# A chain of seven transformer blocks: the end of each block cut by token halves, and the next block begun on the first half

## What is computed

```
x = layer_norm(ALPHA * x + 0.5 * swiglu(x, gate, up, down))    # "ffn1"
mix = rwkv7_mix(x @ w_in)  or  stick_breaking_mix(x @ w_in), with memory_attention
x = layer_norm(ALPHA * x + heads @ w_out)                      # output stage
x = layer_norm(ALPHA * x + 0.5 * swiglu(x, gate, up, down))    # "ffn2"

def layer_norm(x, g, b):
    mu, var = mean(x), mean((x - mu)**2)
    return (x - mu) * rsqrt(var + 1e-5) * g + b                # over the 1024 channels
```

## Time and profile before

| | us |
|---|---|
| median of 3 runs | 1715.24 (1713.86 to 1715.44) |
| the profiled execution | 1710.65 |
| its span, first to last instruction | 1709.0 |
| PE busy in the span | 1482.6 (87%) |
| DVE, ACT, POOL busy | 1030.7, 677.7, 221.7 |
| mean granted TensorE clock | 0.924 |

### The profile page before, as it was taken

One profiled execution on the slowest core, in us unless ns is written; L12 is line 12 of the kernel. 1 busy time (PEld: TensorE's weight loads), 2 busy tenths in 40 slices (PEclk: granted clock), 3 DMA queues, 4 the chain that ended last, 5 costly groups with the idle time before them and its releaser, 6 DMA issues. The chain is left out here.

```text
span 1709.0 us, 29899 instructions
## 1 busy us (share of the span) xinstructions
PE 1482.6 (87%) x11905; PEld 1351.6 (79%) x11905; DVE 1030.7 (60%) x1264; ACT 677.7 (40%) x826; POOL 221.7 (13%) x213
## 2 busy tenths in 40 slices
PE   6768698999899997883886899979999796789996
PEld 5564577999799996883885799979999795589996
DVE  5499956666655556567554655565555646465555
ACT  3355155444443333553232333334333345233332
POOL 0067202222110002101221100001000002110000
PEclk9889788999999998996998899989999898789998
DMA  9655444666476663420003566637666341366661
GB/s 300 195 170 185 142 136 136 185 184 184 123 215 185 186 187 104 149 99 1 4 3 123 173 184 184 185 110 225 186 186 189 99 148 50 123 181 187 185 186 47
DMA packets 318908, 257.42 MB, mean 151 GB/s; under 512 B 7089, under 2 KB 298487, under 8 KB 318839
## 3 DMA queue, kind: packets, MB, share of 16 engines
q1 hardware_dynamic: 318839, 256.44, 49.9%
HBM read 255.36 MB, written 1.05 MB: 150 GB/s over the span
## 5 line engine op out<-in xcount | busy, mean ns | idle before, releaser
L133 PE MATMUL ps<-actT,a_parts 128*128 128x256 f32 x2192 | 634.2, 289 | 51.0 <-DVE a_parts L118 30.1
L134 PE MATMUL ps<-actT,a_parts 128*128 128x256 f32 x2192 | 631.1, 288 | 0.0
L135 PE MATMUL ps<-actT,a_parts 128*128 128x256 f32 x2192 | 630.4, 288 | 0.0
L133 PEld LDWEIGHTS ps<-actT,a_parts 128*128 128x128 f32 x2192 | 432.0, 197 | 62.4 <-issue 33.0
L134 PEld LDWEIGHTS ps<-actT,a_parts 128*128 128x128 f32 x2192 | 432.1, 197 | 3.9
L135 PEld LDWEIGHTS ps<-actT,a_parts 128*128 128x128 f32 x2192 | 431.6, 197 | 0.0
L969 DVE TENSOR_TENSOR a_parts<-a_raw,a_parts 128x2048 fp32r<-128x2048 f32 x100 | 240.4, 2404 | 76.7 <-ACT a_parts L966 76.7
L980 DVE TENSOR_TENSOR b_parts<-b_raw,b_parts 128x1024 fp32r<-128x1024 f32 x80 | 98.1, 1226 | 173.9 <-ACT b_parts L977 173.9
L118 DVE TENSOR_TENSOR a_parts<-a_raw,a_parts 128x2048 fp32r<-128x2048 f32 x54 | 127.3, 2361 | 106.0 <-ACT a_parts L114 105.9
L966 ACT ACTIVATE a_parts<-a_raw 128x2048 fp32r<-128x2048 f32 x100 | 190.0, 1900 | 0.5 <-DMA a_raw<-in_ffn_w_up 0.5
L977 ACT ACTIVATE b_parts<-b_raw 128x1024 fp32r<-128x1024 f32 x100 | 105.7, 1057 | 185.8 <-PE ps L135 185.8
(11 more groups left out here) (305 smaller groups left out, 1634.8 us busy)
## 6 DMA issues: line engine op xcount, KB each, us to landing
a_raw<-in_ffn_w_gate SPq DMA_DIRECT2D x88, 512.0 KB, 3.9
a_raw<-in_ffn_w_up SPq DMA_DIRECT2D x88, 512.0 KB, 5.1
b_raw<-in_ffn_w_down SPq DMA_DIRECT2D x88, 512.0 KB, 3.5
arena<-in_mod_w SPq DMA_DIRECT2D x22, 1024.0 KB, 5.4
a_raw<-in_f_up_w SPq DMA_DIRECT2D x44, 512.0 KB, 5.0
b_raw<-in_f_down_w SPq DMA_DIRECT2D x22, 512.0 KB, 3.5
a_raw<-in_rwkv_w_in SPq DMA_DIRECT2D x10, 1024.0 KB, 5.2
a_raw<-in_sb_w_in SPq DMA_DIRECT2D x10, 1024.0 KB, 5.1
```

The costliest lines, as they stand in the source:

```text
L133: pe.matmul(out, lhs[0], rhs[0], start=start, stop=False)
L134: pe.matmul(out, lhs[0], rhs[1], start=False, stop=False)
L135: return pe.matmul(out, lhs[1], rhs[0], start=False, stop=stop)
```

## The change

In words, for each of the seven ends:

- The last two hidden tiles of an FFN are taken out of the loop, and their `down` products are ordered so that `acc[0]` is complete after 15 of the 24 last matmuls (18 of 24 before). In the output stage chunks 2 and 3 are used for half 0 first, then for half 1, and the transposes of half 0 stand before the last six matmuls.
- The norm on DVE makes only (y - mean) * rstd (`norm_scaled`). Scale and offset are applied behind the transpose, where a channel is a partition: four tiles on ACT and four on DVE for each half, into scratch, and then the split (`tokens_act`, `tokens_dve`). The scale and offset columns of all six norms are loaded with the other parameters in the prologue (three more small DMAs on SP).
- Half 1's statistics, transposes and split move into the next block. The next block starts on half 0: its first two chunks are used twice, for 128 tokens at a time, with half 1's eight transposes between, so 192 matmuls that move 128 columns stand for 96 that move 256. In the RWKV projections the two narrow chunks become one of 256 columns.
- Since `x_tok` now lacks scale and offset, the residual applies them on POOL: two TENSOR_TENSOR and one TENSOR_SCALAR over 2048 columns (`residual`), from rows that SP loads at the start of the stage.
- The last FFN stores the result in two halves. It needs two pairs of rows, its input's and its own, in the same buffer, so SP waits for `xs` before it loads the second pair; this wait stands ahead of the loop of weight loads.

```diff
+        def tokens_dve(dve, t, i, h32, norm):
+            dve.wait_ge(token_turned[t], i + 1)
+            w, src = slice(t * P, (t + 1) * P), turned_tok[t]
+            if norm is not None:
+                for k in range(4, KD):
+                    ins = dve.tensor_scalar(h32[:, k], src[:, k], col("ln_g", norm * KD + k),
+                                            col("ln_b", norm * KD + k), ALU.mult, ALU.add)
+                dve_steps.step(dve, ins)
+                src = h32
+            dve_steps.step(dve, dve.tensor_copy(actT[:, 0, 4:KD, w], src[:, 4:KD]))
+            dve.tensor_tensor(actT[:, 1, 4:KD, w], src[:, 4:KD], actT[:, 0, 4:KD, w].bitcast(F32),
+                              ALU.subtract).then_inc(token_lo[t], 1)
+            dve.wait_ge(token_hi[t], i + 1)
+            dve.tensor_tensor(actT[:, 1, 0:4, w], src[:, 0:4], actT[:, 0, 0:4, w].bitcast(F32),
+                              ALU.subtract).then_inc(token_lo[t], 1)
...
+        def residual(pool, xs, norm, i, rows_at):
...
+            pool.wait_ge(rows_loaded, rows_at)
+            wide = lambda s: rows[:, s].unsqueeze(1).to_broadcast([P, NT, D])
+            pool_steps.step(pool, pool.tensor_tensor(xs, x_tok[:], wide(0), ALU.mult))
+            pool_steps.step(pool, pool.tensor_tensor(xs, xs, wide(1), ALU.add))
+            pool.tensor_scalar(xs, xs, ALPHA, None, ALU.mult).then_inc(pool_out.up("xs"), 1)
...
-                    up_pe(pe, 0, 0)
-                    up_pe(pe, 1, 0)
+                    if got is None:
+                        up_pe(pe, 0, 0)
+                        up_pe(pe, 1, 0)
+                    else:
+                        up_pe(pe, 0, 0, 0)
+                        turn_tokens(pe, 1, got)
+                        up_pe(pe, 1, 0, 0)
+                        up_pe(pe, 0, 0, 1)
+                        up_pe(pe, 1, 0, 1)
...
+                    if last:
+                        sp.wait_ge(pool_out.sem, pool_out.at("xs"))
+                        load_row(sp, 0, norm_row("g", norm))
+                        load_row(sp, 1, norm_row("b", norm))
...
+                    for c in range(2, 4):
+                        ring_a.wait_split(pe, g0 + c)
+                        ins = down_chunk(pe, g0 + c, 0, [2 * c, 2 * c + 1])
                     ins.then_inc(acc_ready.up(0), 1)
+                    down_chunk(pe, g0 + 2, 1, [4, 5]).then_inc(ring_a.used, 1)
+                    down_chunk(pe, g0 + 3, 1, [6])
+                    turn_tokens(pe, 0, hand)
+                    down_chunk(pe, g0 + 3, 1, [7]).then_inc(ring_a.used, 1)
```

More of the change, by code:

```diff
@@ L955, in _ @@
                         ring_b.load(sp, g)
+                    if last:
+                        for t in range(NT):
+                            sp.wait_ge(turn_ready[t], got + 2)
+                            sp.dma_start(out[0, t * P:(t + 1) * P, :], x_tok[:, t]).then_inc(out_stored, 16)
                 def count(ring_first, q, j, back=0):
@@ new lines, in ffn_stage, with second_act, second_dve @@
+            if last:
+                return None
+            if not conv:
+                return second_tokens(hand, yb, norm)
+            def second_act(act):
+                tokens_act(act, 1, hand, None, None)
+            def second_dve(dve, between):
+                dve.tensor_tensor(x_tok[:, 1], x_tok[:, 1], yb[:, 1], ALU.add).then_inc(turn_ready[1], 1)
+                between(dve)
+                tokens_dve(dve, 1, hand, None, None)
+            return second_act, second_dve, hand, None
```

504 lines of the change are left out of this document (287 added, 217 removed).

## The result

The changed kernel takes 1846.72 us (median of 4 runs), the kernel before 1714.55: ratio 1.0796, 95% interval 1.0728 to 1.0864. It is 132 us slower. The prediction said slower, but 1766 us, with a range that ended at 1800; it missed the size by a factor of two and a half. The profiled execution's span is 1845.2 us against 1709.0.

A forecast was written before the change was run, and what follows sets the result against it. Bodies were taken as bound by PE, block ends by DVE's norm. Losses 64+6+9+1 less gains 27.3 and 1.5 gave 51 us more: 1766 us against the median 1715.24, chance 0.66, range 1714 to 1800.

The forecast's parts named there:

- Term 5's last sentence: After each restart, PE's clock stays down 3 to 6 us before, and PE idles as long in pieces now: no difference.
- Rival (d): At the restarts, the clock stays down through the halves because PE's array is half empty: about 1858 us, chance 0.08.
- Term 2, the width: At six restarts, 192 matmuls of 128 columns at 0.115 us replace 96 of 256 at 0.120: 64 us lost.
- (a): Rival: in the halves weight loads hide after all, 0.066 us per matmul, last FFN stalls 18: 1718 us, chance 0.12.
- (b): Rival: halves at 0.066 us per matmul and the last stage's weights not late: 1700 us, chance 0.04.
- (c): Rival: the halves' 128-column matmuls run at plain fp32's rate, 0.213 us warm: 1870 us, chance 0.10.
- Term 3, half 1's transposes: Eight transposes now stand between matmuls of a busy PE, about 1.0 us warm each time: 6 us lost.
- fast halves: Behind the restart, half 1's remaining work is covered by slow matmuls; if they were fast, it would be late by a few us.
- Term 1, the earlier restart: At block ends: 5.5 us won at three FFNs, 1.5 conv FFN, 3.8 and 3 output stages, 2.5 RWKV; 27.3 in all.
- Term 4, SP in the last FFN: SP issues the last FFN's first weight loads only after POOL's xs: stall 7 us plus clock 1.5, 9 us lost.
- Term 5's ends of the program: Storing the result in two halves wins 1.5 us; three more parameter loads in the prologue lose 1.
- POOL and DVE slow each other: In stages other than the last FFN, a split took 2.9 us instead of 2.3 beside POOL, covered by PE's slow start.

The follow-up runs named there:

- before_halves: Kernel before with only the first two chunks of each block (RWKV: three) computed in two passes over 128 tokens; nothing starts earlier: 1884.9 us.
- warm_pool: `after_warm` with POOL's residual in the FFNs begun only behind DVE's last part of half 1's tokens: 1773.1 us.
- halves_warm: `before_halves` plus extra identity matmuls in PE's idle time around the transposes: median 1859.3 us, between two groups of runs.
- after_warm: Changed kernel plus extra identity matmuls in PE's idle time ahead of half 0's transposes and between those and the first half matmul: 1803.0 us.
- full_pool_plain: `full_width` with the FFNs' residual behind half 1's tokens, output stages' residual without gain and offset, conv FFN's chunk 1 split behind the affine step: 1754.9 us.
- full_width: Changed kernel with the next block's first two chunks kept at 256 tokens, begun behind half 1's transposes: 1778.0 us.
- warm_mid: `after_warm` with each plain FFN's residual begun after eight hidden tiles, and SP's rows of the last FFN behind its weights: 1757.1 us.

## Why the prediction was wrong

- **Term 5's last sentence, "PE's clock ... I put no difference", is the step that failed.** It took the granted clock after a restart for a property of the idle time ahead of it. It is as much one of what follows: full-width matmuls left the low clock 3 to 6 us behind the restart (stretches of 10 to 17 us, counted from its fall in the gap), the halves stayed in it as long as they lasted, stretches of 51 to 55 us in `before_halves`, unless something else raised it. With the clock up (`warm_pool`) the same six ends take 171 us, 183 with the extra matmuls ahead of the transposes, against 276 in the changed kernel: **92 us** are the low clock and the stalls that brought it back.
- **Rival (d) foresaw this, and got 0.08.** It gave 1858 against 1847 measured. Its reason, an array half empty, no run tested, and that its number is so near is in part luck: the clock rose inside the halves at four ends (from the first start to the last they took 223 us, not the 245 of `before_halves`), and about as much was lost elsewhere. I held it down with the RWKV row, 88 us of 64x64 matmuls at 1.00. Those are other matmuls; how many of the array's rows and columns they use says nothing on how a stream of the halves' kind fares. The row nearest to the disputed stream was the low stretch behind the restart, and I read it only for its length. What a matmul costs there stands in the trace of the kernel before, behind ffn1 of layer 0:

```profile
674.38 0.41 PE L134 MATMUL ps<-actT,a_parts 128*128 128x256 f32 x1
674.59 0.41 PE L135 MATMUL ps<-actT,a_parts 128*128 128x256 f32 x1
674.80 0.41 PE L133 MATMUL ps<-actT,a_parts 128*128 128x256 f32 x1
```

  At the low clock 256 columns are 0.21 us apart, just as the halves are with 128. So a cut in two costs a second 0.213 there, 20.4 us for 96 matmuls; at full clock 0.120 becomes 2 x 0.112.
- **Term 2, the width**, was right in kind and size: 0.109 to 0.115 us apart at full clock, 9.9 us an end measured in `halves_warm` for 10.6 forecast. The 81 ns quoted from the Trainium skill ("TensorE: Matmul & The Clock Gate", section Back-to-back issue gap) stands there beside measurements in bf16; no run here shows it for fp32r. Rivals (a), (b) and (c) fall with the spacing.
- **Term 3, half 1's transposes**, was right: from the first start to the last, halves with the eight between take 22.20 us (`warm_pool`) and without them 21.35 (`halves_warm`, clock up), 5 us over six ends for 6. That fast halves would wait for half 1 by a few us was right too: 3.2 to 4.8 in `after_warm`.
- **Term 1, the earlier restart**: 6.1, 5.6 and 6.1 us at the three ends with a norm behind an FFN for 5.5 forecast, and 3.0 at the conv FFN for 1.5. But E there was 6 us late (1 in the prologue), and part of it is an order I overlooked: ACT splits chunk 1 ahead of the affine step, 1.8 us in `full_pool_plain`. The output stages failed: from a stage's start to the restart 37.9 became 37.4 us in the first, 38.3 became 41.2 in the second, 0.5 won and 2.9 lost for 3.8 and 3 won. The wait of 2.49 us in the RWKV projections is gone, as forecast. POOL took 4.62, 6.55 and 7.29 us for the residual in stage 0, where rows gave 16.8 in all, and half 0's sum waited for it:

```profile
972.77 7.29 POOL L457 TENSOR_SCALAR arena<-arena 128x2048 f32<-128x2048 f32 x1
...
980.09 1.23 DVE L401 SCALAR_TENSOR_TENSOR arena<-ps,arena 128x1024 f32<-128x1024 f32 x1 [5.26 <-POOL arena L457]
```

  A split of the weights beside it took 3.48 us instead of 2.29 and PE waited 2.86 us for it. The step priced POOL's work alone, and not how POOL and DVE's splits slow each other.
- **Term 4, SP in the last FFN**: in the changed kernel nothing, since the slow halves cover it, as the text said of rival (c); POOL's three operations took 14.7 us there for 16.8. Where the halves were fast or gone it was 10.9 us with POOL's late start and 3.0 with its early one (`full_width`), for 7. Term 5's ends of the program came out: 1.4 won behind the last down matmul for 1.5, 1.1 lost ahead of the first FFN for 1.
- **"POOL and DVE slow each other ... again under PE's slow start"** was mis-sized. The evidence was a split of 2.9 instead of 2.3 beside one operation of 5.4. Beside three operations of 15 us or more, DVE's lost up to 5 us each: 4.8 us a body in `warm_mid`, and stalls of PE behind which the clock fell for some 24 us, of 3.0 and 1.8 us at two ends of the changed kernel and of 3.2 to 4.8 at three of `after_warm`.

As a sum from the changed kernel down: the clock and POOL's place at the ends -74 (to 1773), the residual and SP out of the last FFN's way -16, gain and offset off POOL in the FFNs -12; 30 are left, of which some 10 are the output stages and the conv FFN's order. The rest, some 20, is what is left of the idea with the clock up: the ends cost 22 us more than before, since 192 halves and eight transposes take 22.5 us where 96 full ones took 14 with their low start (11.7 without), and the restart is only 2.5 to 6 earlier. Repaired, the change is still slower, which the forecast's own terms 1 and 2 had said.

What stays open: what decides whether the clock falls once it is up, and whether eight transposes raise it. And the kernel before with extra matmuls gained only 4 us of the 8 to 13 that were expected from the low clock; where the rest goes was not settled.

## What to carry to other kernels

Before a stream of matmuls is cut into thinner ones, look at the granted clock where it starts. If it starts low, price the pieces at the low clock, where here 128 columns cost as much as 256, and ask what would raise it; a PE that is busy all the time is no proof that it will rise, and a short dense stretch put in ahead (here 16 matmuls of the identity, 5.3 us) is a cheap test. And work moved to POOL is not free because POOL is idle: price it by what DVE does in the same time, operand by operand, SBUF or PSUM.

## What the runs showed of the hardware that I had not expected

- 128-column fp32r matmuls with fresh weights, 0.213 us apart, left the granted clock at 0.50 for up to 54.6 us; 32 records of fp32 matmuls of the identity (5.29 us) raised it at four of four places, and the same stream then ran at 0.109 to 0.115.
- At a granted clock of 0.50 fp32r matmuls of 256 and of 128 columns were both 0.213 us apart; at 1.00 they were 0.120 and 0.112.
- With the clock at 1.00 at their start, the same halves kept it at six of six ends in `warm_pool` and `warm_mid` and lost it at four of six in `halves_warm`, whose runs fell into two groups, 1840 and 1880 us. PE's pause ahead of them was 0.45 to 0.53 us in the first two kernels and 1.74 in the third.
- DVE beside POOL: a cast of 0.43 us took 4.17 (`full_width`), one of 0.29 took 5.01 and a split of 2.29 took 6.69 (`warm_mid`), where all operands are in SBUF; 1.37 stayed 1.37 where the input is in PSUM.
- Matmuls queued behind the last useful instruction of a block delay the other engines' next block: ACT began 1.6 us behind PE's transposes instead of 0.3.
